# PEER stage of a diffusion layer on one core: three kinds of token tiles, one pass over v, gate rows on VectorE

## Chip, core and metric

The kernel runs on one core of one Trainium2 chip, in one launch. The metric is device microseconds of that core. All data are float32; large matrix products are done in three products of a high and a low part in fp32r. Matmuls run on TensorE, elementwise work on VectorE and ScalarE, row gathers are issued by GpSimd, all other transfers by SyncE's queue (SP).

## What is computed

The layer mixes tokens (neighbourhood attention beside a bidirectional recurrence) and then mixes channels in a PEER layer: each of 1024 tokens chooses, in each of 8 heads, 16 of 128 x 128 experts by product keys. An expert is a row of `u` and a row of `v`. Only this second part is changed.

```python
def peer(h, w_q, keys, u, v):
    q = (h @ w_q).reshape(B, S, PEER_HEADS, 2, PEER_HALF)
    s = jnp.einsum('bshpd,hpkd->bshpk', q, keys).astype(jnp.float32)
    top_s, top_i = lax.top_k(s, PEER_TOPK)
    cand_s = (top_s[..., 0, :, None] + top_s[..., 1, None, :]).reshape(B, S, PEER_HEADS, PEER_TOPK * PEER_TOPK)
    cand_i = (top_i[..., 0, :, None] * PEER_NKEYS + top_i[..., 1, None, :]).reshape(B, S, PEER_HEADS, PEER_TOPK * PEER_TOPK)
    best_s, pos = lax.top_k(cand_s, PEER_TOPK)
    expert = jnp.take_along_axis(cand_i, pos, axis=-1)
    gate = jax.nn.softmax(best_s, axis=-1).astype(h.dtype)
    def chunk(args):
        hc, ec, gc = args
        act = jax.nn.gelu(jnp.einsum('td,thkd->thk', hc, u[ec]))
        return jnp.einsum('thk,thkd->td', gc * act, v[ec])
```

## The kernel before

The 1024 tokens are 8 tiles of 128. Six tiles are **dense**: for them all 16384 experts are computed as matrix products, and the gates, zero for experts not chosen, pick the sum. Two tiles are **gathered**: each token's 128 chosen rows of u and of v are fetched one choice at a time (one indirect DMA on GpSimd brings one row of 1024 numbers to each of 128 tokens, 512 KB) and VectorE multiplies and sums them. `keep.y` holds the sum of a gathered tile.

Four stages run one behind the other, with all engines meeting between them: norms and attention, recurrence, merge with the routing projections (`project_and_route`, which leaves each tile's best scores and places in HBM), and then the two that matter here.

**Select** (`activate_and_select`) walks over 128 chunks of u, each the 128 experts that share a first index. For a chunk, SP loads u_raw (two buffers), ScalarE writes its high part u_hi, VectorE its low part u_lo (L1683), both in rings of three, and TensorE runs 48 matmuls of 384 tokens for the six dense tiles; ScalarE's gelu writes `a`, which goes to `act_scratch`. Beside that, by a schedule written out by hand (a lead of 12 chunks, six bodies of 18, a rest of 8), VectorE makes each tile's final choice in 8 parts (`Choice.part`), TensorE turns it, VectorE makes one-hot rows of it (`one2`, L1687, and `one1`, L1691, which carries the gate), and TensorE multiplies them in groups of four tokens into ps_g, the dense gates (L1895): 32 groups a tile, four in each of 8 chunks of a body. ScalarE copies them to `gm`, and SP stores them. VectorE also takes the rows of one gathered tile: 128 dot products with rows of u (L1806) and 128 additions of rows of v (L1810). Each frees one of four row buffers, for which GpSimd's next gather waits (L1620).

**Combine** (`combine`) walks over the 128 chunks of v twice, for three dense tiles each time, since 3 tiles x 2 halves are six of the eight PSUM banks. For a chunk, SP loads activations, gates and v_raw; VectorE multiplies gates by activations (L2035); ScalarE and VectorE make v_hi, v_lo (L2037), wa_hi and wa_lo (L2039); TensorE runs 18 matmuls of 512 columns into ps_y. Rings have four buffers: ScalarE's copy to v_hi waits until TensorE is done with the chunk four before. In pass 1 VectorE takes one u row of the second gathered tile per chunk (L2044), in pass 2 one v row (L2050); GpSimd fetches them (L1997). At the end of a pass the banks are copied out, turned and added to the residual (`finish`, L2063), 8 pieces a pass.

## Time and profile before

| what | us |
|---|---|
| median of three runs (3873.61 to 3875.75) | 3874.95 |
| span of the profiled execution | 3878.8 |
| select, first to last u matmul starts | 1524.0 to 2784.5 |
| combine, first to last v matmul starts | 2799.4 to 3868.4 |
| TensorE busy in the span | 3642.9 |
| VectorE busy | 2626.6 |
| GpSimd busy | 611.8 |

The profile is one execution; its span is 3.9 us above the median. Busy time counts overlapping instructions once, and consecutive instructions of one engine overlap a little: what one costs its engine is the distance to the start of the next. A matmul of 512 columns is listed with 0.39 us, though one begins every 0.23 us.

### The profile page before, as it was taken

How to read it: one execution, taken by the hardware profiler on the slowest of the kernel's cores; microseconds unless marked ns; L12 is line 12 of the kernel's file. 1: busy time of each engine (PE TensorE's matmuls, PEld its weight loads, DVE VectorE, ACT ScalarE, POOL GpSimd, SP SyncE). 2: the span in 40 equal slices, each digit the busy share in tenths (PEclk: the TensorE clock that was granted, in tenths of full speed). 3: DMA queues.
4: the chain of work that ended last, by engine and by line, in shares of the span. 5: the costliest groups of instructions: out<-in, count | busy, mean ns of one | idle time of the engine just before them, and what ended most of it. 6: DMA issues, size and time to landing. Idle time of an engine off the chain costs nothing. (4 is left out here: it accounts for less than half of the span.)

```text
span 3878.8 us, 57008 instructions
## 1 busy us (share of the span) xinstructions
PE 3642.9 (94%) x20360; PEld 3195.4 (82%) x20360; DVE 2626.6 (68%) x5328; ACT 1271.2 (33%) x1760; POOL 611.8 (16%) x516
## 2 busy tenths in 40 slices
PE   5899999799599896999999999999899999999999
PEld 2777777687487796999999999999878888878887
DVE  5134443488533786577878888888588888878887
ACT  3133343377311311222322232323233333333332
POOL 0000000000000000222232323132122222332221
PEclk8999999899799998999999999999999999999999
DMA  7311110111333112667777869595899999999997
GB/s 281 136 61 59 49 56 28 52 58 38 123 117 126 54 51 78 207 214 234 264 261 237 285 211 306 190 333 166 278 387 352 354 353 355 323 378 353 353 353 255
DMA packets 372666, 811.48 MB, mean 209 GB/s; under 512 B 30704, under 2 KB 207728, under 8 KB 369008
## 3 DMA queue, kind: packets, MB, share of 16 engines
q1 hardware_dynamic: 298736, 540.29, 39.8%
q0 software_dynamic: 73728, 268.47, 20.0%
q8 instruction: 130, 2.13, 0.2%
q14 instruction: 72, 0.59, 0.0%
HBM read 679.14 MB, written 129.50 MB: 208 GB/s over the span
## 5 line engine op out<-in xcount | busy, mean ns | idle before, releaser
L80 PE MATMUL s_ps_a<-back_dense_hi,s_u_hi 128*128 128x384 f32 x2048 | 703.2, 343 | 30.4 <-DVE s_u_lo L1683 30.4
L82 PE MATMUL s_ps_a<-back_dense_hi,s_u_lo 128*128 128x384 f32 x2048 | 686.2, 335 | 0.0
L81 PE MATMUL s_ps_a<-back_dense_lo,s_u_hi 128*128 128x384 f32 x2048 | 685.8, 335 | 0.0
L80 PE MATMUL c_ps_y<-c_v_hi,c_wa_hi 128*128 128x512 f32 x1536 | 601.1, 391 | 28.0 <-DVE c_wa_lo L2039 27.7
L81 PE MATMUL c_ps_y<-c_v_lo,c_wa_hi 128*128 128x512 f32 x1536 | 599.8, 391 | 0.0
L82 PE MATMUL c_ps_y<-c_v_hi,c_wa_lo 128*128 128x512 f32 x1536 | 599.6, 390 | 0.0
L2005 ACT ACTIVATE c_v_hi<-c_v_raw 128x1024 fp32r<-128x1024 f32 x256 | 271.5, 1060 | 633.3 <-PE c_ps_y L82 585.5
L1620 POOL DMA_INDIRECT s_row<-in_u_rows,back_expert x128 | 159.6, 1247 | 2004.2 <-DVE back_expert L1785 1582.7
L2037 DVE TENSOR_TENSOR c_v_lo<-c_v_raw,c_v_hi 128x1024 fp32r<-128x1024 f32 x256 | 313.4, 1224 | 181.8 <-ACT c_v_hi L2005 180.2
L80 PEld LDWEIGHTS s_ps_a<-back_dense_hi,s_u_hi 128*128 128x128 f32 x2048 | 386.1, 189 | 30.5 <-DVE s_u_lo L1683 30.5
L81 PEld LDWEIGHTS s_ps_a<-back_dense_lo,s_u_hi 128*128 128x128 f32 x2048 | 386.2, 189 | 0.0
L82 PEld LDWEIGHTS s_ps_a<-back_dense_hi,s_u_lo 128*128 128x128 f32 x2048 | 385.2, 188 | 0.0
L80 PEld LDWEIGHTS c_ps_y<-c_v_hi,c_wa_hi 128*128 128x128 f32 x1536 | 289.8, 189 | 89.8 <-DVE c_v_lo L2037 29.2
L82 PEld LDWEIGHTS c_ps_y<-c_v_hi,c_wa_lo 128*128 128x128 f32 x1536 | 289.7, 189 | 60.7
L81 PEld LDWEIGHTS c_ps_y<-c_v_lo,c_wa_hi 128*128 128x128 f32 x1536 | 289.9, 189 | 60.0
L1683 DVE TENSOR_TENSOR s_u_lo<-s_u_raw,s_u_hi 128x1024 fp32r<-128x1024 f32 x128 | 156.5, 1223 | 239.1 <-ACT s_u_hi L1639 223.4
L1643 ACT ACTIVATE s_a<-s_ps_a 128x768 f32<-128x768 f32 x128 | 103.9, 812 | 501.0 <-PE s_ps_a L82 487.8
L1657 ACT ACTIVATE s_gm<-s_ps_g 128x512 f32<-128x512 f32 x192 | 114.8, 598 | 399.0 <-PE s_ps_g L1895 399.0
L1620 POOL DMA_INDIRECT s_row<-in_v,back_expert x128 | 171.7, 1342 | 413.1 <-DVE back_y L1810 398.4
L1895 PE MATMUL s_ps_g<-s_one 128*128 128x128 f32 x1536 | 206.7, 277 | 6.7 <-DVE s_one L1691 6.7
L1691 DVE TENSOR_SCALAR s_one<-s_iota,s_sel_t 128x128 f32<-128x128 f32 x768 | 212.7, 349 | 0.0
L1895 PEld LDWEIGHTS s_ps_g<-s_one 128*128 128x128 f32 x1536 | 195.3, 191 | 20.6 <-DVE s_one L1691 20.4
(331 smaller groups left out, 6723.9 us busy)
## 6 DMA issues: line engine op xcount, KB each, us to landing
c_v_raw<-in_v SPq DMA_DIRECT2D x256, 512.0 KB
s_u_raw<-in_u SPq DMA_DIRECT2D x128, 512.0 KB
act_scratch<-s_a SPq DMA_DIRECT2D x128, 384.0 KB
gm_scratch<-s_gm SPq DMA_DIRECT2D x48, 1024.0 KB
c_a<-act_scratch SPq DMA_DIRECT2D x256, 192.0 KB
c_g<-gm_scratch SPq DMA_DIRECT2D x256, 192.0 KB
a_w<-in_w_ada SPq DMA_DIRECT2D x24, 1024.0 KB, 7.5
gate_scratch<-at_gate SPq DMA_DIRECT2D x32, 256.0 KB, 2.0
```

The lines of the kernel that those rows point to most:

```text
L80: nc.tensor.matmul(out, w_hi, x_hi, start=first, stop=False)
L81: nc.tensor.matmul(out, w_hi, x_lo, start=False, stop=False)
L82: return nc.tensor.matmul(out, w_lo, x_hi, start=False, stop=last)
L1620: gp.indirect_dma_start(out=row[:, n % R], out_offset=None, in_=io["u_rows"] if n < SEL else io["v_rows"], in_offset=bass.IndirectOffsetOn ...
L1643: nc.scalar.activation(a[:, s].rearrange("p (h t) -> p h t", h=2), ps_a[:, s, :, 0:W], ACT.Gelu_apprx_tanh).then_inc(act_done, 1)
L1657: nc.scalar.activation(gm[:, :, g * GT:(g + 1) * GT], ps_g[:, g % 2].rearrange("p (i t) -> p i t", t=GT), ACT.Copy).then_inc(g_copied, 1)
L1683: nc.vector.tensor_tensor(u_lo[:, n], u_raw[:, s], u_hi[:, n].bitcast(F32), ALU.subtract).then_inc(u_lo_done, 1)
L1691: last = nc.vector.tensor_scalar(one1[:, g % 2, i], iota[:], sel_t[:, 0, t:t + 1], sel_t[:, 2, t:t + 1], ALU.is_equal, ALU.mult)
L1895: last = nc.tensor.matmul(ps_g[:, g % 2].rearrange("p (n t) -> p n t", t=GT)[:, :, i], one2[:, g % 2, i], one1[:, g % 2, i], start=True, s ...
L2005: nc.scalar.activation(v_hi[:, s], v_raw[:, s], ACT.Copy).then_inc(v_hi_done, 1)
L2037: nc.vector.tensor_tensor(v_lo[:, s], v_raw[:, s], v_hi[:, s].bitcast(F32), ALU.subtract).then_inc(v_lo_done, 1)
```

## The change

The tiles are now of three kinds. Tiles 0 to 3 are dense in both stages (`BOTH = 4`). Tiles 4 and 5 are dense in select (their activations are among the 768 columns), but in combine their v rows are gathered: GpSimd looks up each chosen expert's activation with an indirect DMA of one 4-byte number a token from `act_scratch` (index `keep.place`), VectorE multiplies these by the gates (`weights`) and adds the rows (`unit`). Tiles 6 and 7 are gathered in both, and both of them now wholly in select: 2 x 128 dots, then 2 x 128 additions, by turns for the two tiles, with six row buffers.

Combine has one pass over v, with 4 tiles x 2 halves on all eight banks; v_hi, v_lo, wa_hi and wa_lo lie in the space of the dense tokens, which nobody needs any more. Gates are stored in blocks of 32 tokens and loaded for eight chunks at a time. All loops are written out. Select's work is placed by `selection_plan`, a table that gives each chunk its parts of choices, its gate groups and its number of rows. The end turns and finishes 16 pieces. `project_and_route` stores the choices tile by tile, in the order of `CHOICES`.

```diff
+BOTH = 4
+LOOKED = DENSE - BOTH
+TB = BOTH * P
+CHOICES = (6, 0, 7, 1, 2, 3, 4, 5)
...
-            for first, end, turn in ((DENSE, DENSE + 1, 0), (0, DENSE, 1), (DENSE + 1, TT, DENSE + 1)):
-                sp.dma_start(io["best_scr"][:, turn:turn + end - first], all_best[:, first:end]).then_inc(chosen_stored, 16)
...
+            for n, tile in enumerate(CHOICES):
+                sp.dma_start(io["best_scr"][:, n], all_best[:, tile]).then_inc(chosen_stored, 16)
...
+def selection_plan():
+    parts, turn, groups, rows = ([[] for _ in range(NK)] for _ in range(4))
+    begin = {0: (0, 2), 1: (4, 2), 2: (10, 1), 3: (20, 0.5), 4: (44, 0.5), 5: (72, 0.5), 6: (92, 0.5), 7: (108, 0.5)}
...
+    for g in range(BOTH * GROUPS):
+        groups[10 + g * 113 // (BOTH * GROUPS)].append(g)
+    units, taken = 2 * GATHERED * SEL, 0
+    span = [8.3 + 1.02 * len(groups[c]) for c in range(NK)]
+    other = [1.3 + 3.4 * len(parts[c]) + 2.15 * len(groups[c]) for c in range(NK)]
+    share = (sum(other) + 1.32 * units) / sum(span)
+    for c in range(NK):
+        fit = int((sum(span[:c + 1]) * share - sum(other[:c + 1])) / 1.32)
+        upto = units if c == NK - 1 else min(units, max(fit, taken)) if c >= 5 else 0
+        rows[c] = list(range(taken, upto))
+        taken = upto
+    return parts, turn, groups, rows, ends
...
+            for c in range(NK):
+                for d in turn[c - 1] if c >= 1 else ():
+                    turned_in(d)
+                for g in groups[c + 1] if c + 1 < NK else ():
+                    plain_rows(g)
+                first = len(rows[c]) // 2
+                for n in rows[c][:1]:
+                    unit(n)
+                if c + AHEAD < NK:
+                    low(c + AHEAD)
+                for n in rows[c][1:first]:
+                    unit(n)
+                for n, j in parts[c]:
+                    part(n, j)
+                for n in rows[c][max(first, 1):]:
+                    unit(n)
...
+            def look_up(b):
+                for n in range(b * BATCH, (b + 1) * BATCH):
+                    t, k = n % LOOKED, n // LOOKED
+                    gp.indirect_dma_start(out=looked[:, t, k:k + 1], out_offset=None, in_=table,
+                                          in_offset=bass.IndirectOffsetOnAxis(ap=keep.place[:, t, k:k + 1], axis=0)).then_inc(look_in[b % PHASES], 16)
...
+                    if n >= R:
+                        gp.wait_ge(used, n - R + 1)
...
+            look_up(0)
+            look_up(1)
+            for b in range(BATCHES):
+                fetch(b)
+                if b + 2 < BATCHES:
+                    look_up(b + 2)
...
+        units_upto = [0 if c < FIRST else UNITS * (c - FIRST + 1) // row_chunks for c in range(NK)]
...
+                nc.vector.tensor_tensor(spans, g[:, b % 2, :, i], spans, ALU.mult).then_inc(gated, 1)
+                dve.wait_ge(v_hi_done, c + 1)
                 nc.vector.tensor_tensor(v_lo[:, s], v_raw[:, s], v_hi[:, s].bitcast(F32), ALU.subtract).then_inc(v_lo_done, 1)
...
+                for n in here[:1]:
+                    unit(n)
+                dve.wait_ge(wa_hi_done, c + 1)
+                nc.vector.tensor_tensor(wa_lo[:, s], a[:, s], wa_hi[:, s].bitcast(F32), ALU.subtract).then_inc(wa_lo_done, 1)
+                for n in here[1:]:
+                    unit(n)
```

In combine `BATCH` is 16, `R` is 8, `FIRST` is 3, and `used` counts the rows that VectorE has added.

GpSimd's whole work in the two stages (s_ names a tile of select, c_ one of combine). Before:

```order
L1620 DMA s_row<-in_u_rows,back_expert 128x1024 x128
L1620 DMA s_row<-in_v,back_expert 128x1024 x128
L1512 UNCONDITIONAL_BRANCH
L1992 UNCONDITIONAL_BRANCH
L1997 DMA c_row<-in_u_rows,back_expert 128x1024 x128
L1997 DMA c_row<-in_v,back_expert 128x1024 x128
```

After, to the third batch of rows:

```order
L1634 DMA s_row<-in_u_rows,back_expert 128x1024 x256
L1634 DMA s_row<-in_v,back_expert 128x1024 x256
L1539 UNCONDITIONAL_BRANCH
L1958 UNCONDITIONAL_BRANCH
L1965 DMA c_looked<-act_scratch,back_place 128x1 x32
L1973 DMA c_row<-in_v,back_expert 128x1024 x16
L1965 DMA c_looked<-act_scratch,back_place 128x1 x16
L1973 DMA c_row<-in_v,back_expert 128x1024 x16
L1965 DMA c_looked<-act_scratch,back_place 128x1 x16
L1973 DMA c_row<-in_v,back_expert 128x1024 x16
```

256 gathers moved from combine to select, and combine got 256 look-ups between 256 row gathers, 32 of them ahead of the first row.

VectorE in combine, from one row to the next chunk's gate product, before (c_g is gates, c_v_lo and c_wa_lo the low parts):

```order
L2044 SCALAR_TENSOR_TENSOR c_row,c_dots<-c_row,c_tok 128x1024
L2035 TENSOR_TENSOR c_g<-c_g,c_a 128x384
L2036 REGISTER_ALU
L2037 TENSOR_TENSOR c_v_lo<-c_v_raw,c_v_hi 128x1024
L2039 TENSOR_TENSOR c_wa_lo<-c_g,c_wa_hi 128x384
```

and after, in chunks 3 and 4 (back_dense_lo and back_dense_hi now hold the low and high parts):

```order
L2031 TENSOR_TENSOR c_a<-c_g,c_a 128x512
L2033 TENSOR_TENSOR back_dense_lo<-c_v_raw,back_dense_hi 128x1024
L2002 TENSOR_TENSOR c_w<-c_looked,back_gate 128x2x8
L2014 SCALAR_TENSOR_TENSOR c_y<-c_row,c_w,c_y 128x1024
L2039 TENSOR_TENSOR back_dense_lo<-c_a,back_dense_hi 128x512
L2014 SCALAR_TENSOR_TENSOR c_y<-c_row,c_w,c_y 128x1024
L2031 TENSOR_TENSOR c_a<-c_g,c_a 128x512
```

A chunk carries two rows instead of one, and the first of them stands ahead of the low part that TensorE waits for.

VectorE in select, in a chunk with gate groups, before (s_one is one2 and one1):

```order
L1683 TENSOR_TENSOR s_u_lo<-s_u_raw,s_u_hi 128x1024
L1687 TENSOR_TENSOR s_one<-s_iota,s_sel_t 128x512
L1691 TENSOR_SCALAR s_one<-s_iota,s_sel_t 128x128 x4
L1804 ISA
L1806 ISA
L1806 SCALAR_TENSOR_TENSOR s_row,s_dots<-s_row,s_tok 128x1024
L1686 REGISTER_ALU
L1687 TENSOR_TENSOR s_one<-s_iota,s_sel_t 128x512
L1691 TENSOR_SCALAR s_one<-s_iota,s_sel_t 128x128 x4
```

and after, a chunk with one group and six rows:

```order
L1694 TENSOR_TENSOR s_one<-s_iota,s_sel_t 128x512
L1699 TENSOR_SCALAR s_one<-s_iota,s_sel_t 128x128 x4
L1803 SCALAR_TENSOR_TENSOR s_row,s_dots<-s_row,s_tok 128x1024
L1680 TENSOR_TENSOR s_u_lo<-s_u_raw,s_u_hi 128x1024
L1803 SCALAR_TENSOR_TENSOR s_row,s_dots<-s_row,s_tok 128x1024 x5
```

The groups, four in eight chunks of eighteen before, now stand one or two in every chunk from 10 to 122, made one chunk ahead of their matmuls.

## Rows read from the trace of the kernel before

**Rows 1.** The page's first line.
```profile
span 3878.8 us, 57008 instructions
```
**Rows 2.** Stages by tile: duration ns min/median/max, first and last start; who waited.
```profile
L80 PE MATMUL s_ps_a<-back_dense_hi,s_u_hi x2048: 334/334/689, 1524.0 to 2784.5; 128*128 128x384 f32 x187
...
L80 PE MATMUL c_ps_y<-c_v_hi,c_wa_hi x1536: 389/389/767, 2799.4 to 3867.9; 128*128 128x512 f32 x192
...
L82 PE MATMUL c_ps_y<-c_v_hi,c_wa_lo x1536: 387/389/628, 2800.4 to 3868.4; 128*128 128x512 f32 x192
...
  ACT c_v_hi L2005: 585.5, 228
```
**Rows 3.** Windows: length, busy us of PE, PEld, DVE, ACT, POOL; clock, DMA share, GB/s.
```profile
1524.00:2785.00 1261.00, 1254.26 (x7698) 1240.10 (x7698) 980.33 (x2137) 356.93 (x472) 331.36 (x256) 1.00 0.73 241
2800.00:2860.00 60.00, 53.79 (x219) 43.50 (x218) 46.52 (x73) 21.57 (x29) 14.24 (x15) 0.92 1.04 411
2820.00:2824.00 4.00, 0.07 (x1) 0.10 (x1) 1.91 (x3) 2.08 (x3) 0.00 (x0) 0.87 1.05 409
2824.00:2829.00 5.00, 5.00 (x12) 3.94 (x13) 5.00 (x9) 2.27 (x4) 1.59 (x2) 0.50 1.04 411
2900.00:3300.00 400.00, 400.00 (x1766) 331.24 (x1765) 324.28 (x491) 144.41 (x196) 99.23 (x98) 1.00 0.99 354
```
**Rows 4.** Timeline of VectorE in select: start us, us, what; idle before.
```profile
1545.19 1.23 DVE L1683 TENSOR_TENSOR s_u_lo<-s_u_raw,s_u_hi 128x1024 fp32r<-128x1024 f32 x1 [3.72 <-ACT s_u_hi L1639]
...
1553.51 1.22 DVE L1683 TENSOR_TENSOR s_u_lo<-s_u_raw,s_u_hi 128x1024 fp32r<-128x1024 f32 x1 [4.80 <-ACT s_u_hi L1639]
...
1716.04 1.23 DVE L1683 TENSOR_TENSOR s_u_lo<-s_u_raw,s_u_hi 128x1024 fp32r<-128x1024 f32 x1 [2.38 <-ACT s_u_hi L1639]
1717.18 0.68 DVE L1687 TENSOR_TENSOR s_one<-s_iota,s_sel_t 128x512 f32<-128x512 f32 x1
...
1718.81 1.22 DVE L1806 SCALAR_TENSOR_TENSOR s_row<-s_row,s_tok 128x1024 f32<-128x1024 f32 x1
...
1728.38 1.22 DVE L1683 TENSOR_TENSOR s_u_lo<-s_u_raw,s_u_hi 128x1024 fp32r<-128x1024 f32 x1 [2.31 <-ACT s_u_hi L1639]
```
**Rows 5.** Timeline of VectorE in combine, one chunk without waits.
```profile
2824.85 0.55 DVE L2035 TENSOR_TENSOR c_g<-c_g,c_a 128x384 f32<-128x384 f32 x1
2825.32 1.22 DVE L2037 TENSOR_TENSOR c_v_lo<-c_v_raw,c_v_hi 128x1024 fp32r<-128x1024 f32 x1
2826.45 0.55 DVE L2039 TENSOR_TENSOR c_wa_lo<-c_g,c_wa_hi 128x384 fp32r<-128x384 f32 x1
2826.92 1.22 DVE L2044 SCALAR_TENSOR_TENSOR c_row<-c_row,c_tok 128x1024 f32<-128x1024 f32 x1
...
2828.07 0.55 DVE L2035 TENSOR_TENSOR c_g<-c_g,c_a 128x384 f32<-128x384 f32 x1
```
**Rows 6.** Timeline of GpSimd (POOL) at the start of combine, and beside VectorE in select.
```profile
2790.91 0.94 POOL L1997 DMA_INDIRECT c_row<-in_u_rows,back_expert  x1 [0.30 <-issue]
...
1854.22 1.22 DVE L1806 SCALAR_TENSOR_TENSOR s_row<-s_row,s_tok 128x1024 f32<-128x1024 f32 x1
1854.57 1.68 POOL L1620 DMA_INDIRECT s_row<-in_u_rows,back_expert  x1 [4.43 <-DVE s_row L1806]
...
1855.36 2.28 DVE L1723 TENSOR_REDUCE s_sel<-s_work 128x128 f32<-128x2048 f32 x1
1856.55 0.94 POOL L1620 DMA_INDIRECT s_row<-in_u_rows,back_expert  x1 [0.30 <-issue]
```
**Rows 7.** Groups by line, GpSimd: busy us, mean ns, idle before and releasers.
```profile
L1620 POOL DMA_INDIRECT s_row<-in_v,back_expert x128 | 171.7, 1342 | 413.1 <-DVE back_y L1810 398.4 <-issue 12.5 <-DVE s_row L1806 2.1
L1620 POOL DMA_INDIRECT s_row<-in_u_rows,back_expert x128 | 159.6, 1247 | 2004.2 <-DVE back_expert L1785 1582.7 <-DVE s_row L1806 404.6 <-issue 17.0
```
**Rows 8.** Timeline of GpSimd in pass 2, one of a series of like rows.
```profile
3420.97 2.61 POOL L1997 DMA_INDIRECT c_row<-in_v,back_expert  x1 [0.66 <-DVE c_y L2050]
```
**Rows 9.** Timeline of the end: the eight finishes of VectorE.
```profile
3870.46 5.91 DVE L2063 SCALAR_TENSOR_TENSOR c_x<-c_ps_t,keep_mod,c_x 128x512 f32<-128x512 f32 x8 [0.95 <-PE c_ps_t L2127]
```
**Rows 10.** Timeline of SP's queue, one of six stores ending `project_and_route`.
```profile
1508.01 0.46 SPq L1300 DMA_DIRECT2D best_scratch<-p_x  x1
```

More of the change, by code:

```diff
@@ L1506, in activate_and_select @@
     W = TD // 2
-    LEAD_UNITS = 8
-    UNITS = [4 if j == PARTS or j >= HOT_END else 2 for j in range(BODY)]
-    PER_BODY = sum(UNITS)
-    HALF_BODIES = DENSE // 2
-    assert LEAD_UNITS + HALF_BODIES * PER_BODY == SEL and LEAD_UNITS == REST
+    UNITS = GATHERED * SEL
+    parts, turn, groups, rows, ends = selection_plan()
+    chunk_of = {g: c for c in range(NK) for g in groups[c]}
+    blocks = BOTH * P // SPAN
+    PER_BLOCK = SPAN // GT
     with ExitStack() as ctx:
@@ L1614, in _ @@
+            for b in range(2):
+                sp.wait_ge(a_stored[b], 16 * (NK // 2))
+                sp.wait_ge(g_stored[b], 16 * (blocks // 2))
         @block.gpsimd
         def _(gp):
-            gp.wait_ge(step, STEPS)
-            for n in range(2 * SEL):
+            for n in range(2 * UNITS):
+                if n < UNITS:
+                    g, k, table = n // SEL, n % SEL, io["u_rows"]
+                else:
+                    g, k, table = n % GATHERED, (n - UNITS) // GATHERED, io["v_rows"]
+                if n < UNITS and k == 0:
+                    gp.wait_ge(step, BEFORE[CHOICES.index(DENSE + g) + 1])
@@ L1842, in _ @@
-            for c in range(AHEAD):
-                lo(c, 0)
-            nc.vector.memset(keep.y[:], 0.0).then_inc(y_zero, 1)
-            dve.wait_ge(consts_in, 32)
-            choice = Choice(0, 0)
-            rows = Rows(0, 0, None)
-            for j in range(LEAD):
-                if j < PARTS:
-                    choice.part(j)
-                else:
-                    dve.wait_ge(tok_in, 16)
-                    rows.take(LEAD_UNITS // (LEAD - PARTS), True)
-                lo(j + AHEAD, 0)
@@ new lines, in selected @@
+            def selected(d):
+                pe.wait_ge(step, BEFORE[DENSE_CHOICES[d] + 1])
+                if d >= 1:
+                    pe.wait_ge(turned, d)
+                for r in range(3):
+                    last = nc.tensor.transpose(ps_t[:, r * P:(r + 1) * P], sel[:, r], ident[:])
+                last.then_inc(t_ready, 1)
+            pe.wait_ge(consts_in, 48)
+            for c in range(NK):
+                for q in range(4):
+                    quarter(c, q)
+                    if q == 1:
+                        for d in turn[c]:
+                            selected(d)
+                    if q in (1, 3):
+                        for g in groups[c][q // 2:q // 2 + 1]:
+                            gates(g)
@@ L1992, in _ @@
+            for k in range(KD):
+                for j in range(2):
+                    sp.wait_ge(out_done, 2 * k + j + 1)
+                    sp.dma_start(io["out"][:, k * T + j * HALF:k * T + (j + 1) * HALF], x1[j][:, k]).then_inc(stored, 16)
+            sp.wait_ge(stored, 16 * 2 * KD)
         @block.gpsimd
         def _(gp):
-            for n in range(2 * SEL):
-                if n >= RING:
-                    gp.wait_ge(used, n - RING + 1)
-                gp.indirect_dma_start(out=row[:, n % RING], out_offset=None, in_=io["u_rows"] if n < SEL else io["v_rows"],
-                                      in_offset=bass.IndirectOffsetOnAxis(ap=keep.expert[:, 1, n % SEL:n % SEL + 1], axis=0)).then_inc(row_in[n % RING], 16)
+            table = io["act_scr"].rearrange("c p (t o) -> (c p t) o", o=1)
@@ L2064, in finish @@
+            def finish(k, j):
+                n = 2 * k + j
+                dve.wait_ge(turned, n + 1)
+                nc.vector.scalar_tensor_tensor(out=x1[j][:, k], in0=ps_y[:, n % BANKS], scalar=keep.mod[:, 5 * KD + k:5 * KD + k + 1], in1=x1[j][:, k],
                                                op0=ALU.mult, op1=ALU.add).then_inc(out_done, 1)
             nc.vector.memset(y[:], 0.0).then_inc(y_zero, 1)
-            with dve.Fori(0, NK // RING) as i:
-                for s in range(RING):
-                    chunk(0, i, RING * i + s, s)
-                    dot(i, bass.ds(RING * i + s, 1), s)
```

843 lines of the change are left out of this document (357 added, 486 removed).

## The prediction

> **What bounds the kernel now.** I read the page's first lines, then where the two expert stages begin and end, then single stretches. The span is 3878.8 us [rows 1]. The select stage's matmuls run from 1524.0 to 2784.5, the combine stage's from 2799.4 to 3868.4, and in the latter ScalarE waits 585.5 us for TensorE to free a ring slot [rows 2]: data is there, TensorE is the bound. The windows agree: TensorE is busy for 400 of 400 us in the middle of combine, 1766 matmuls, 0.2265 us each; in select it is busy 1254 of 1261 us and VectorE 980 us [rows 3]. In select a chunk of u without gate matmuls takes 8.32 us (from one u_lo to the next), one with four gate groups 12.34 us, so a group of four gate matmuls costs TensorE 1.01 us [rows 4]. GpSimd only issues row gathers, one for each of 512 rows, and mostly waits for VectorE.
>
> **Part 1, combine on TensorE.** Before: two passes over v, 18 matmuls a chunk, 4608 in all. After: one pass, 4 tiles x 2 halves x 3 products = 24 a chunk, 3072. At 0.2265 us a chunk takes 5.44 us, the pass 696 us. If TensorE stayed the bound, this alone would take 1536 x 0.2265 = 348 us away.
>
> **Part 2, what must keep up in combine.** VectorE: starts of successive instructions give 0.47 us for 384 columns, 1.13 for 1024 and 1.15 for a row [rows 5]; 512 columns interpolate to 0.60. A chunk is gate product 0.60, v_lo 1.13, wa_lo 0.60 and 2.05 rows at 1.15, in sum 4.7 us, below 5.44. ScalarE's two copies a chunk are the same pieces of work, on an engine that waited before. Transfers: v 67.1 MB, activations 33.6, gates 33.6, 256 rows 134.2, x1 4.2, in sum 272.6 MB. Over 696 us that is 392 GB/s. The trace moves 411 GB/s over 60 us with the DMA share at 1.04, and 354 where it was only asked for that [rows 3]; at 411 the bytes take 663 us. 32768 look-ups of 4 bytes come on top. So DMA lies 0 to 5% below TensorE's pace, without air.
>
> The Trainium skill (DMA: Bandwidth & Descriptors, Specifications) gives some 358 GB/s as the limit of HBM for one core. By it the bytes would take 272.6 / 0.358 = 761 us, an estimate; this trace's 411 GB/s speak against it as a ceiling when one core runs.
>
> **Part 3, GpSimd in combine, where I choose.** It issued 256 gathers in 1079 us and now issues 512 (256 rows and 256 look-ups, one for each selected expert of tiles 4 and 5) in one queue, in batches of 16 and 16; I take a look-up to cost it what a row does, as both name 128 indices. Alone, a gather takes 0.94 us plus 0.30 us to the next, 1.24 [rows 6]. Beside VectorE it takes longer: one issued at 1854.57 into a row product that began at 1854.22 took 1.68 us, one issued beside a reduction with a single SBUF input 0.94 [rows 6]. The slow one ends 0.81 us after the end of that product, as if it had been let in only then; the product has two SBUF inputs. Over the 256 gathers of select the means are 1.247 and 1.342 us [rows 7], so 1.6 us from one to the next when nothing else holds it.
> All of VectorE's work in a combine chunk has two SBUF inputs, and it would be busy 4.7 of 5.44 us, about as much as in select. A pair of row and look-up then takes 3.2 us, while TensorE wants one in 5.44 / 2.05 = 2.65. So **GpSimd becomes the bound**. The ends: 2.48 us a pair if no gather waits, and 6.54 us if every one behaves like the stretch with 3.27 us each [rows 8]. I take 3.2, since select is the nearest stretch in VectorE's load; my own range for it is 2.9 to 3.6.
>
> The Trainium skill says the same in part (SBUF — State Buffer, Who interferes with whom): a VectorE instruction with two SBUF inputs contends with a GpSimd one that reads SBUF, and the later one blocks. It adds the inference that such instructions leave descriptor writing alone; by that a pair would stay near 2.5 us and TensorE would be the bound. The 1.68 us row speaks for a delay.
>
> The stage, from its first DMA issue (2789.2 before):
> - 32 look-ups ahead of the first row, 32 x 1.24 = 40 us. VectorE reaches a row in chunk 3 and TensorE stands there until about 46, but GpSimd is the one that counts.
> - 14 rounds of 16 rows and 16 look-ups, 448 x 1.6 = 717 us. VectorE needs 16 x 2.3 = 37 us of the 51 in a round. TensorE idles up to 9 us a round. Behind 4 us without matmuls (2820 to 2824) its granted clock was 0.50, that is 1.2 GHz, from 2824 to 2829 [rows 3]; a fall of 7 us a round costs 3 to 4 us, which still fits into 51.
> - the last 32 rows, no longer between look-ups, at VectorE's pace of 2.3 us: 74 us; about 4 us for a landing (an estimate, from 0 to 8) and 5.4 for TensorE's last chunk.
> Sum 40 + 717 + 74 + 9 = 840 us, where before it was 3868.6 - 2789.2 = 1079. **Combine: -239.**
>
> **Part 4, the end.** 16 banks instead of 8 are finished in a row behind the last matmul; 8 took 5.91 us [rows 9]. **+6.** The old finish in the middle of pass 2 is already in part 3's difference.
>
> **Part 5, select.** Only 4 tiles get gate rows: 128 groups for 192, so 64 x 1.01 = 65 us less on TensorE; 1261 becomes 1196. VectorE loses 64 x 1.63 = 104 us and gains 256 rows x 1.15 = 294 (tile 7's rows move here from combine): 980 + 190 = 1170 of 1196 us, 98%. Counting `selection_plan`'s table by these prices, no chunk leaves VectorE more than some 12 us behind, and u_lo is two chunks (17 us) ahead, so most of it is covered. What isn't: in chunks with two groups VectorE waits up to 5 us for TensorE's gates; 5.3 rows a chunk at 1.6 us ask 8.5 of GpSimd's 9.3 us; the last five chunks carry 31 rows, at 1.6 us 50 us where TensorE needs 42. Transfers are 419 MB, 351 GB/s. I give back 15 us. **Select: -50** (0 to -65).
>
> **Part 6, small ones.** 16 DMAs for 6 store the choices behind the last top-16, 0.46 us each [rows 10]: +4. The first gate load of combine is 2.1 MB; that is hidden behind the 32 look-ups, and would cost 3 us if they were not there. Start of select: +1.
>
> **Sum.** 3878.8 - 239 + 6 - 50 + 5 = 3601. The median of three runs, 3874.95, is 3.9 us below the profiled span; so 3597.
>
> **Rivals.**
> - *TensorE and DMA set combine, GpSimd hides.* For: GpSimd's 0.94; VectorE stands still when it lacks a row and then lets gathers pass. Against: the means of select. Stage: 46 us until chunk 3, then 125 x 5.44 = 680, and 0 to 35 us for DMA that runs at its limit: 726 to 761, against 1079 a gain of 318 to 353. Total 3483 to 3520. With 358 GB/s in place of 411 the stage is 761 + some 10 for the start, total 3530.
> - *Select loses its balance.* VectorE at 98% with waits on rows. Against: the two chunks of lead. If it runs 5% over its 1170 and combine is as forecast, total 3640; with GpSimd at 1.9 us a gather in combine as well (448 x 0.3 = 134) 3775.
> - *Slower than before: every gather waits behind a whole VectorE round.* Place: combine's row fetches. At 3.27 us each [rows 8], 512 take 1674 us, and the total is near 4500. It decides from (1079 + 39 - 123) / 448 = 2.2 us a gather on (the 39 us are what parts 4 to 6 save, 123 the parts of the stage not in the 448). For: a whole series of such gathers. Against: they stand only where VectorE had no gap at all; a starved VectorE has gaps.
> - *The change doesn't do what it says*: it is written out, nothing is left to a scheduler; below 1%.
>
> **Chances.** Forecast, 3530 to 3690: 0.54. TensorE or DMA bound, 3480 to 3530: 0.28. Select or GpSimd worse, 3690 to 3865: 0.14. Slower: 0.03. Within 0.2% (about what a measurement of this kernel can tell from no change): 0.01. So faster 0.96. The range 3475 to 3700 takes in the first two cases and a little of the third, about 0.83.
>
> **What would show it.** GpSimd busy over 75% in combine, its idle times "issue" and not VectorE's release; VectorE waiting for c_row; TensorE in combine busy about 83%, with the granted clock at half after gaps; last matmul some 840 us after the stage's first DMA. If instead ScalarE still waits for TensorE and gathers last 0.94 to 1.0 us, the rival has it. In select: matmuls over 1196 to 1215 us, few waits of TensorE for one-hot rows or u_lo. I am wrong above all if a look-up costs GpSimd or the DMA engines something else than a row.

## The result and the profile after

The changed kernel takes 3747.09 us (median of four runs, 3739.56 to 3749.73), the kernel before beside it 3875.35: a ratio of 0.9666, 95% interval 0.9652 to 0.9679, 128 us faster. The forecast was 3597, 278 us faster, with a range that ended at 3700. The direction was right, more than half of the gain did not come, and the time lies outside the range.

The profiled execution's span is 3737.8 us; the forecast in its terms was 3601, so 137 us are missing. (It is the fastest of the four: by the medians 150 are missing. What follows accounts for the 137.) The page's first line, then a row of the tile view of select (as in [rows 2]), then the windows of the two stages (as in [rows 3]):

```profile
span 3737.8 us, 47042 instructions
```

```profile
L84 PE MATMUL s_ps_a<-back_dense_hi,s_u_hi x2048: 333/334/689, 1521.3 to 2796.5; 128*128 128x384 f32 x187
```

```profile
1521.00:2797.00 1276.00, 1212.15 (x7180) 1203.93 (x7180) 1158.41 (x2193) 316.29 (x409) 719.78 (x505) 0.97 0.89 326
2900.00:3600.00 700.00, 568.17 (x2367) 463.92 (x2366) 473.10 (x509) 155.46 (x196) 572.90 (x411) 0.89 0.80 300
```

Select did not shrink: 1276 us, where [rows 2] give 1261. TensorE is busy for 1212 of it, VectorE for 1158 instead of 980. In combine TensorE is busy 568 of 700 us; GpSimd is busy 573, and with 0.30 us of issue before each of its 411 instructions (123 us) that fills the 700. The granted clock there is 0.89 for 1.00 before.

The end of select and the start of combine (timeline: VectorE's last row sums, ScalarE's last gelu, SP's first loads; the counterparts before were at 2785.27 and 2789.22):

```profile
2795.86 6.53 DVE L1814 SCALAR_TENSOR_TENSOR back_y<-s_row,s_w,back_y 128x1024 f32<-128x1024 f32 x5 [1.24 <-DMA s_row<-in_v,back_expert]
2797.26 0.81 ACT L1670 ACTIVATE s_a<-s_ps_a 128x768 f32<-128x768 f32 x1 [7.75 <-PE s_ps_a L86]
...
2804.55 6.42 DVE L1814 SCALAR_TENSOR_TENSOR back_y<-s_row,s_w,back_y 128x1024 f32<-128x1024 f32 x5 [0.56 <-DMA s_row<-in_v,back_expert]
2811.81 2.50 DVE L1814 SCALAR_TENSOR_TENSOR back_y<-s_row,s_w,back_y 128x1024 f32<-128x1024 f32 x2 [0.84 <-DMA s_row<-in_v,back_expert]
2816.56 0.37 SPq L1931 DMA_DIRECT2D c_g<-gm_scratch  x1
```

TensorE is through with u at 2796.9, VectorE still has some dozen rows to add, and combine's first load goes out 19.7 us after the last matmul instead of 4.3.

Groups by line (busy us, mean ns, idle before and its releasers): VectorE's rows in both stages, GpSimd's gathers (as in [rows 7]).

```profile
L1814 DVE SCALAR_TENSOR_TENSOR back_y<-s_row,s_w,back_y 128x1024 f32<-128x1024 f32 x256 | 319.2, 1281 | 49.3 <-DMA s_row<-in_v,back_expert 48.9
L1803 DVE SCALAR_TENSOR_TENSOR s_row<-s_row,s_tok 128x1024 f32<-128x1024 f32 x256 | 305.3, 1220 | 49.2 <-DMA s_row<-in_u_rows,back_expert 48.5
L2014 DVE SCALAR_TENSOR_TENSOR c_y<-c_row,c_w,c_y 128x1024 f32<-128x1024 f32 x256 | 326.7, 1278 | 262.9 <-DMA c_row<-in_v,back_expert 262.6
L1973 POOL DMA_INDIRECT c_row<-in_v,back_expert x256 | 389.0, 1520 | 80.1 <-issue 76.2 <-DVE c_y L2014 3.9
L1965 POOL DMA_INDIRECT c_looked<-act_scratch,back_place x256 | 332.7, 1300 | 87.0 <-issue 77.7 <-POOLq L1539 9.2
```

In combine GpSimd waits for VectorE 3.9 us in all, and VectorE waits 262.9 for rows: GpSimd's queue sets the stage, as forecast. In select VectorE waits 98.5 us for rows. That was not forecast. 1158, 98.5 and 16.5 for u_hi add up to 1273 of the stage's 1276.

The loss in select isn't spread out. From the first matmul of one chunk of u to that of the next, the 98 chunks with one gate group have a median of 9.23 us, those without a group 8.32 and those with two 10.04. The 127 such distances are 96 us longer than these prices add up to, and 94 of the 96 lie in 23 chunks. The longest, 21.0 us in the ninth chunk, is no wait for rows: TensorE stands there for the first tile's choice, which VectorE is still making (view of waits for TensorE in select: us in all, times, longest).

```profile
PE s_ps_t L1869 <- DVE s_sel L1787: 18.5, 4, 10.5
```

Where the 137 us lie: combine from its first load to its last matmul 906.0 for 840 (+66); select 1275.6 for 1211 (+65); the way from select's last matmul to combine's first load 19.7 for 4.3 (+15); the end 15.2 for 16.4 (-1); select's start 1521.3 for 1529 (-8).

### The profile page after: what moved, and what is told of

It reads as the page before. It is cut to its first block and busy times, and to the rows that moved or that the text cites. A ratio compares the mean times of both kernels' runs of the same rounds, so it can differ in the third digit from the quotient of the medians.

```text
span 3737.8 us, 47042 instructions
## 1 busy us (share of the span) xinstructions
PE 3276.6 (88%) x18306; PEld 2887.7 (77%) x18306; DVE 2580.4 (69%) x4897; ACT 1054.7 (28%) x1438; POOL 1450.4 (39%) x1028
## 5 line engine op out<-in xcount | busy, mean ns | idle before, releaser
L84 PE MATMUL c_ps_y<-back_dense_hi 128*128 128x512 f32 x1024 | 415.2, 406 | 190.7 <-DVE back_dense_lo L2039 190.7
L2014 DVE SCALAR_TENSOR_TENSOR c_y<-c_row,c_w,c_y 128x1024 f32<-128x1024 f32 x256 | 326.7, 1278 | 262.9 <-DMA c_row<-in_v,back_expert 262.6
L1634 POOL DMA_INDIRECT s_row<-in_v,back_expert x256 | 375.8, 1468 | 240.4 <-DVE back_y L1814 181.9
L1973 POOL DMA_INDIRECT c_row<-in_v,back_expert x256 | 389.0, 1520 | 80.1 <-issue 76.2
L85 PE MATMUL c_ps_y<-back_dense_lo,back_dense_hi 128*128 128x512 f32 x1024 | 411.6, 402 | 0.0
L86 PE MATMUL c_ps_y<-back_dense_hi,back_dense_lo 128*128 128x512 f32 x1024 | 410.7, 401 | 0.0
L1965 POOL DMA_INDIRECT c_looked<-act_scratch,back_place x256 | 332.7, 1300 | 87.0 <-issue 77.7
L1814 DVE SCALAR_TENSOR_TENSOR back_y<-s_row,s_w,back_y 128x1024 f32<-128x1024 f32 x256 | 319.2, 1281 | 49.3 <-DMA s_row<-in_v,back_expert 48.9
L1803 DVE SCALAR_TENSOR_TENSOR s_row<-s_row,s_tok 128x1024 f32<-128x1024 f32 x256 | 305.3, 1220 | 49.2 <-DMA s_row<-in_u_rows,back_expert 48.5
L85 PEld LDWEIGHTS c_ps_y<-back_dense_lo,back_dense_hi 128*128 128x128 f32 x1024 | 201.3, 197 | 42.2
```

The source lines that it names most:

```text
L84: nc.tensor.matmul(out, w_hi, x_hi, start=first, stop=False)
L85: nc.tensor.matmul(out, w_hi, x_lo, start=False, stop=False)
L86: return nc.tensor.matmul(out, w_lo, x_hi, start=False, stop=last)
L1634: gp.indirect_dma_start(out=row[:, n % R], out_offset=None, in_=table, in_offset=bass.IndirectOffsetOnAxis(ap=keep.expert[:, g, k:k + 1], ...
L1803: nc.vector.scalar_tensor_tensor(out=row[:, n % R], in0=row[:, n % R], scalar=1.0, in1=tok[:, g], op0=ALU.mult, op1=ALU.mult, accum_out=do ...
L1814: nc.vector.scalar_tensor_tensor(out=keep.y[:, g], in0=row[:, n % R], scalar=w[:, g, k:k + 1], in1=keep.y[:, g], op0=ALU.mult, op1=ALU.add ...
```

## Experiments

In all of them "stage" is combine from SP's first load to the last matmul, "step" the mean distance between the starts of the 33rd and the 481st gather, and "select" its first to its last matmul, all from the profiled execution. The changed kernel has 906, 1.72 and 1276 us. Runs that leave a stage as it is show how far these numbers move by themselves: combine 897 to 913 us with a step of 1.70 to 1.73 and 75 to 90 gathers of over 2 us, select 1269 to 1278.

**1. Combine without look-ups.**

```diff
-            look_up(0)
-            look_up(1)
...
-                if b + 2 < BATCHES:
-                    look_up(b + 2)
...
-                dve.wait_ge(look_in[b % PHASES], 16 * BATCH * (b // PHASES + 1))
-                nc.vector.tensor_tensor(w[:, :, cols], looked[:, :, cols], keep.gate[:, GATHERED:, cols], ALU.mult).then_inc(w_done, 1)
+                nc.vector.tensor_tensor(w[:, :, cols], keep.gate[:, GATHERED:, cols], keep.gate[:, GATHERED:, cols], ALU.mult).then_inc(w_done, 1)
```

> The 256 look-ups of activations in combine are left out (the weights of tiles 4 and 5 are then the gates squared, so their part of the sum is not the reference's). Measured in the changed kernel: the stage takes 906 us from its first SP issue to the last matmul, GpSimd starts one gather every 1.71 us and idles only by issue. Theory 1, GpSimd's queue sets the stage: 256 gathers at about 1.7 us are 435 us, far below TensorE's pace, so TensorE or the transfers bound the stage: 125 x 5.44 = 680 plus some 25 for the start and 5 for the end, 710 to 760 us, total 3750 - 170 = about 3580. Rival, TensorE and the 272 MB of transfers set it (the 4-byte look-ups carry no bytes): the stage stays above 870 us, total above 3710.

The stage takes 727 us, the total is 3568.7. Its window:

```profile
2900.00:3500.00 600.00, 600.00 (x2649) 496.82 (x2648) 540.33 (x578) 181.25 (x223) 341.76 (x229) 1.00 1.02 396
```

TensorE is busy for the whole 600 us at the full clock, as in [rows 3], and GpSimd now waits 300.8 us for VectorE to free a buffer. First to last matmul is 705 us, where the 128 chunks of 5.44 that the prediction's rival had for a bound are 696. So the look-ups, one number a token each, cost the changed kernel some 180 us. The run alone doesn't tell GpSimd's time from that of their 32768 descriptors; 396 GB/s with a DMA share of 1.02 in this run, against 300 and 0.80 in the changed kernel, show that the engines that move data were not the limit there, and experiment 2, with as many look-ups and a DMA share of 0.59 over the same 909 us, shows it from the other side. The 396 GB/s over 600 us also settle a point of the prediction: the Trainium skill's 358 GB/s for one core's HBM (DMA: Bandwidth & Descriptors, Specifications), which the page makes by halving a stack's rate between two cores, is no ceiling here, with one core running.

**2. Quarter rows: 128 KB a gather instead of 512, the same instructions.**

```diff
-                gp.indirect_dma_start(out=row[:, n % R], out_offset=None, in_=table,
+                gp.indirect_dma_start(out=row[:, n % R, 0:D // 4], out_offset=None, in_=table,
...
-                    gp.indirect_dma_start(out=row[:, n % R], out_offset=None, in_=io["v_rows"],
+                    gp.indirect_dma_start(out=row[:, n % R, 0:D // 4], out_offset=None, in_=io["v_rows"].rearrange("e (q d) -> (e q) d", q=4),
```

> In both stages every row gather brings 256 numbers a token in place of 1024 (128 KB for 512 KB; the rest of each row buffer is set to zero once, so the gathered sums are wrong); GpSimd issues the same instructions and VectorE works over the same 1024 columns. Select moves 218 MB for 419, combine 172 for 273. Select: theory 1, full DMA queues delay the loads of u (ScalarE waited 139.5 us for them, 3.4 before) and the rows: select falls from 1276 us to 1200 to 1220. Rival, VectorE's load and its fixed order make the waits: select stays at 1260 to 1276. Combine: theory 1, GpSimd's instruction count sets it: the stage stays at 906 us within 20. Rival, bytes set it: it falls below 840.

Combine: 909 us, of which GpSimd spent 9 waiting for the zeroes, with a step of 1.71. A hundred MB less change nothing. Select: 1203 us, inside the 1200 to 1220 of the first theory and 7 above what the prediction had before it gave 15 back. What became shorter is the landing (DMA issues of select, last number the median us from issue to landing; first the changed kernel, then this one), and with it VectorE's waits (groups of this one):

```profile
s_row<-in_u_rows,back_expert POOLq DMA_INDIRECT x256, 8.0
```

```profile
s_row<-in_u_rows,back_expert POOLq DMA_INDIRECT x256, 4.0
```

```profile
L1817 DVE SCALAR_TENSOR_TENSOR back_y<-s_row,s_w,back_y 128x1024 f32<-128x1024 f32 x256 | 317.6, 1284 | 4.2 <-DMA s_row<-in_v,back_expert 4.1
L1806 DVE SCALAR_TENSOR_TENSOR s_row<-s_row,s_tok 128x1024 f32<-128x1024 f32 x256 | 302.6, 1217 | 12.7 <-DMA s_row<-in_u_rows,back_expert 12.4 <-DVE s_digit L1768 0.2
```

**3. Quarter vector: row products and sums over 256 columns, whole transfers.**

```diff
-                nc.vector.scalar_tensor_tensor(out=y[:, t], in0=row[:, n % R], scalar=w[:, t, k:k + 1], in1=y[:, t],
+                nc.vector.scalar_tensor_tensor(out=y[:, t, 0:D // 4], in0=row[:, n % R, 0:D // 4], scalar=w[:, t, k:k + 1], in1=y[:, t, 0:D // 4],
```

and the same in select's two forms.

> In both stages VectorE's row products and row sums work over 256 columns instead of 1024 (about 0.35 us for 1.15; the gathered sums are wrong), and every transfer is whole. With quarter rows and whole VectorE work select took 1203 us. Theory 1, transfers set what was lost in select: it stays at 1250 to 1276 us although VectorE loses 512 x 0.8 = 410 of its 1158 us. Rival, VectorE's load and order are needed for it as well: select falls to 1200 to 1220 here too. Combine: VectorE's busy time falls by 205 us, so that fewer gathers come up in a two-input instruction: the step falls from 1.72 to 1.4 to 1.6 us and the stage to 780 to 850; if GpSimd doesn't depend on VectorE it stays at 906.

Select falls to 1193 us, so the rival of this text was right: late rows without VectorE's load (1193 us) cost select next to nothing, and neither does the load without late rows (1203 us in experiment 2). VectorE waits even longer for rows here (232 us), but has the time. The loss needs both, an engine without slack and rows that come late to it. Combine falls to 762 us with a step of 1.41: GpSimd's pace hangs on what VectorE does.

**4. Three buffers for u_raw.**

```diff
-        u_raw = m.sb("u_raw", [P, 2, KD, P])
+        u_raw = m.sb("u_raw", [P, 3, KD, P])
...
-                if c + 4 < NK:
-                    u_load(c + 4)
+                if c + 5 < NK:
+                    u_load(c + 5)
```

> Select gets three buffers for u_raw instead of two, and SP asks for a chunk five ahead instead of four; nothing else changes. Theory 1, what costs select its 65 us is the late landing of single loads of u (ScalarE waited for them 139.5 us, up to 5.9 at a time, with the next load asked for only when VectorE had finished with the buffer two before): a third buffer takes most of these waits, select falls from 1276 us to 1215 to 1240, total 3690 to 3715. Rival 1, the queues simply lack throughput in the stretches with six rows a chunk: the loads wait as long as before, select stays within 10 us. Rival 2, it is the rows, not u, on which VectorE falls behind: within 10 us too, but with ScalarE's wait for u gone and VectorE's wait for rows (48.5 and 47.2 us) grown.

3732.66 us, ratio 0.9634 (0.9611 to 0.9656). Select takes 1262 us, 13 less and 7 below the shortest of the runs that leave it alone; ScalarE's waits for u fall from 139.5 us to 35.1, VectorE's for rows from 97 to 84. The late loads of u, the most visible wait in select's view of waits, were a sign of the same slow landings and not the cause. Rival 2 is nearest, though the rows' waits did not grow.

**5. and 6. Four and eight row buffers in select.**

```diff
-    R = 6
+    R = 4
```

> Select's ring of row buffers has 4 in place of 6; nothing else changes. Measured with 6: VectorE is busy 1158 us of select's 1276 and waits 98 us for rows; a row lands 8.0 to 8.4 us after its gather is issued (4.0 to 4.3 with quarter rows, where the waits for rows were 17 us and select 1203). Theory 1, VectorE is the bound of select and loses what it waits for rows, and that wait comes from landing time over the number of buffers: a buffer's turn is about 1.5 (issue) + 8.2 (landing) + 1.2 (VectorE) = 10.9 us, so 6 give a row every 1.8 us at best, 4 one in 2.7; 512 rows then take 1390 us at least where 1276 - 65 us are there for them: select 1400 to 1460 us, total 3870 to 3930. Rival, the lack is in the engines that move the bytes: fewer rows in flight land earlier, and select stays within 30 us of 1276.

```diff
-    R = 6
+    R = 8
```

> Select's ring of row buffers has 8 in place of 6; nothing else changes. Theory 1 (VectorE bounds select, and waits for rows because of landing time over buffers): with 8 a row can come every 1.4 us, VectorE's waits for rows fall from 98 us to 30 to 50, and select from 1276 us to 1215 to 1240; the additions behind the last matmul of u keep their number, so the gap of 19.7 us shrinks by 2 to 5; total 3695 to 3720. Rival, the transfers as a whole are the limit (the queues are busy 0.86 to 0.97 there): two more rows in flight only land later, 9 us and more, u comes later as well, and select stays within 15 us of 1276.

With 4 the total is 3988.7, slower than before the change, and select takes 1506 us. With 8 it is 3675.37 us, ratio 0.9479 (0.9465 to 0.9494), 72 us below the changed kernel, and select takes 1213, two us from the forecast. VectorE's two groups of rows with 4 buffers, then with 8:

```profile
L1814 DVE SCALAR_TENSOR_TENSOR back_y<-s_row,s_w,back_y 128x1024 f32<-128x1024 f32 x256 | 322.2, 1279 | 177.0 <-DMA s_row<-in_v,back_expert 176.4
L1803 DVE SCALAR_TENSOR_TENSOR s_row<-s_row,s_tok 128x1024 f32<-128x1024 f32 x256 | 307.7, 1220 | 157.1 <-DMA s_row<-in_u_rows,back_expert 155.8 <-issue 0.8
```

```profile
L1814 DVE SCALAR_TENSOR_TENSOR back_y<-s_row,s_w,back_y 128x1024 f32<-128x1024 f32 x256 | 318.0, 1280 | 12.2 <-DMA s_row<-in_v,back_expert 9.6 <-issue 1.4 <-DVE back_y L1814 1.1
L1803 DVE SCALAR_TENSOR_TENSOR s_row<-s_row,s_tok 128x1024 f32<-128x1024 f32 x256 | 303.4, 1217 | 22.1 <-DMA s_row<-in_u_rows,back_expert 17.8 <-issue 4.1
```

The waits go 334, 98.5, 34 us with 4, 6 and 8 buffers and select goes with them: 230 us more for 236 more of waiting, 62 less for 64 less. The chunks that take over 1 us more than their price are 64, 23 and 6. The engines that move the bytes had room for it: select's window with 8 reads 343 GB/s at a share of 0.92, where it was 326 at 0.89. The first theory stands, with its numbers off: I had expected select at 1400 to 1460 for 4 buffers and at 1215 to 1240 for 8, with a total of 3695 to 3720 and 2 to 5 us off the gap in front of combine, which lost 1. The gap in front of combine is still 18.6 us; VectorE has 13 sums left behind the last matmul of u, nearly without a wait among them. That part is the place of the rows in `selection_plan`, not their landing.

**7. Combine's v_lo by another instruction.**

```diff
-                nc.vector.tensor_tensor(v_lo[:, s], v_raw[:, s], v_hi[:, s].bitcast(F32), ALU.subtract).then_inc(v_lo_done, 1)
+                nc.vector.scalar_tensor_tensor(out=v_lo[:, s], in0=v_raw[:, s], scalar=1.0, in1=v_hi[:, s].bitcast(F32),
+                                               op0=ALU.mult, op1=ALU.subtract).then_inc(v_lo_done, 1)
```

> In combine VectorE makes v_lo by SCALAR_TENSOR_TENSOR (1.0 times v_raw, minus v_hi) in place of TENSOR_TENSOR: same numbers, same length. In the changed kernel a gather beside no VectorE instruction takes 0.94 us, one that comes up in the row product or in wa_lo 1.4 to 1.5 (it ends 0.81 us after the end of that instruction), and one that comes up in the gate product, with v_lo right behind it, 2.63: it is held through both. There are about 100 of these. Theory 1, only two TENSOR_TENSOR in a row hold a gather through both: the 2.63 turns to 1.5, GpSimd saves 100 x 1.15 = 115 us, less what VectorE's starving takes back; stage 906 to 800 to 840, total 3640 to 3680. Rival, any two instructions with two SBUF inputs back to back can hold it: no change within 10 us.

Ratio 0.964 (0.9622 to 0.9658), stage 888 us, step 1.68. Gathers of over 2 us are 72 instead of 88, and those that meet gate product and v_lo still last 2.63 (median of 84 of them). So the theory falls: with a SCALAR_TENSOR_TENSOR as the second instruction a gather is still held through two. The 18 us, more than the rival's 10, go with a smaller count of the same; of them only 9 lie outside what combine does by itself.

**8. A row between gate product and v_lo.**

```diff
-                dve.wait_ge(v_hi_done, c + 1)
-                nc.vector.tensor_tensor(v_lo[:, s], v_raw[:, s], v_hi[:, s].bitcast(F32), ALU.subtract).then_inc(v_lo_done, 1)
                 here = range(taken, units_upto[c])
                 taken = units_upto[c]
                 for n in here[:1]:
                     unit(n)
+                dve.wait_ge(v_hi_done, c + 1)
+                nc.vector.tensor_tensor(v_lo[:, s], v_raw[:, s], v_hi[:, s].bitcast(F32), ALU.subtract).then_inc(v_lo_done, 1)
```

> In combine VectorE's first row of a chunk stands between the gate product and v_lo in place of behind v_lo; nothing else changes. Theory 1, as for the kernel with v_lo by SCALAR_TENSOR_TENSOR: the gate product is followed by a SCALAR_TENSOR_TENSOR, the gathers of 2.63 us go down to 1.5, and the stage falls from 906 us by up to 115, total 3640 to 3690. Rival 1, the hold isn't of this kind: no change within 10 us. Rival 2, v_lo now stands behind a wait for a row, so that TensorE, which waits for v_lo, stops more often: the stage grows.

Ratio 0.9671 (0.9653 to 0.9688), stage 912 us, 90 gathers of over 2 us. The long ones only moved: they now stand over v_lo and wa_lo, which had come together (1.2 and 0.6 us, 2.63 to the end of the gather as before). No gain.

**9. One SBUF input for gate product, v_lo and wa_lo.**

```diff
-                nc.vector.tensor_tensor(spans, g[:, b % 2, :, i], spans, ALU.mult).then_inc(gated, 1)
+                nc.vector.tensor_copy(spans, g[:, b % 2, :, i]).then_inc(gated, 1)
...
-                nc.vector.tensor_tensor(v_lo[:, s], v_raw[:, s], v_hi[:, s].bitcast(F32), ALU.subtract).then_inc(v_lo_done, 1)
+                nc.vector.tensor_copy(v_lo[:, s], v_raw[:, s]).then_inc(v_lo_done, 1)
```

and wa_lo likewise.

> In combine VectorE's gate product, v_lo and wa_lo become plain copies of one SBUF input (g, v_raw and a), so the numbers are not the reference's; the row sums still have two inputs. Theory 1, an instruction of VectorE with two SBUF inputs holds a gather that comes up in it until its end: the gathers of over 2 us (88 of 512) vanish and only those that meet a row sum last 1.4 to 1.5; the mean falls from 1.41 us to 1.05 to 1.2, the step between gathers from 1.72 to 1.35 to 1.5, and the stage from 906 us to 740 to 800. Rival, what holds a gather is something else that was only beside these instructions (the queue's own room, or transfers): the mean stays at 1.35 or more and the stage above 880. If the copies are much shorter than the operations they replace, part of a gain is their shorter time; the durations by what runs beside a gather tell.

The stage falls to 856 us and the step to 1.61, gathers of over 2 us to 33: 50 us less, where 106 to 166 were expected, and between the two theories' ranges. The timeline says why (VectorE and GpSimd, beside two look-ups):

```profile
2830.14 0.69 DVE L2033 CAST back_dense_lo<-c_v_raw 128x1024 fp32r<-128x1024 f32 x1 [0.24 <-ACT back_dense_hi L1990]
2830.37 1.28 POOL L1965 DMA_INDIRECT c_looked<-act_scratch,back_place  x1 [0.30 <-issue]
...
2831.95 0.95 POOL L1965 DMA_INDIRECT c_looked<-act_scratch,back_place  x1 [0.30 <-issue]
```

The look-up that comes up in the copy, which has one input, ends 0.82 us behind the copy's end, as one behind a product does. The copies also run at nearly double pace (0.69 for 1.22 us). So one input is no protection; these copies only hold a gather more briefly. The Trainium skill (SBUF — State Buffer, Who interferes with whom) says that of copies and casts between places in SBUF in their fast modes, and this run agrees. The same section takes it that a `tensor_tensor` leaves descriptor writing alone; the rows below show a delay, and the measurement decides.

**10. Batches of four in combine; 11. the same and eight row buffers; 12. batches of two and eight row buffers.**

```diff
-    BATCH = 16
+    BATCH = 4
```

> In combine look-ups and rows go in batches of 4 in place of 16: 8 look-ups stand ahead of the first row instead of 32, and 8 rows behind the last look-up instead of 32. Measured before this: 42.8 us for the first 32 gathers, 1.72 us for each of 448, 92.9 us for the last 32 rows and the end (2.9 a row). Theory 1, GpSimd's queue sets the stage by a fixed step: 8 x 1.3 + 496 x 1.72 + 8 x 2.9 = 887 us for 906, total about 3730; less if rows that come evenly let VectorE and TensorE run evenly. Rival, in long batches VectorE stands still during the look-ups and lets them pass at 1.24 us, and with short ones every gather meets a working VectorE: the step grows to 1.85 or more, the stage to 940 or more, total 3780.

3707.31 us, ratio 0.9561 (0.9545 to 0.9577), stage 870 us, step 1.67; the 36 us are about twice what a fixed step gave (19). Gathers of over 2 us are 40 instead of 88.

> Eight row buffers in select, and batches of 4 look-ups and rows in combine: both edits together. They lie in different stages with a meeting of all engines between, so both theories expect their gains to add: combine as with batches of 4 alone, 870 us for 906, and select as with eight buffers alone. With select at 1215 to 1240: total 3650 to 3680; by the rival for select 3700 to 3710.

3646.61 us, ratio 0.9395 (0.9381 to 0.9409): select 1211, stage 876. The gains add, to 100 us where the two alone give 112.

```diff
-    R = 6
+    R = 8
...
-    BATCH = 16
+    BATCH = 2
...
-    PHASES = 4
+    PHASES = 8
```

> Eight row buffers in select, and batches of 2 look-ups and 2 rows in combine, with eight semaphores for the look-ups in place of four. Theory 1: what batches of 4 won (step 1.72 to 1.67, the last 32 gathers and the end 92.9 to 66 us) goes a little further, since 4 rows stand behind the last look-up for 8: combine 860 to 870 us, total 5 to 10 us below the version with batches of 4. Rival: the weights, now 128 small instructions of VectorE in place of 64, each behind a landing, make up for it or more: 0 to 15 us above.

3614.86 us, ratio 0.9322 (0.9307 to 0.9336), the fastest version here and 132 us below the changed kernel. The stage takes 838.5 us with a step of 1.60, and no gather at all lasts over 2 us. GpSimd's two groups in this version (tile view: min/median/max in ns):

```profile
L1973 POOL DMA_INDIRECT c_row<-in_v,back_expert x256: 940/1146/1893, 2762.2 to 3584.8; - x128
...
L1965 POOL DMA_INDIRECT c_looked<-act_scratch,back_place x256: 943/1433/1970, 2757.2 to 3577.9; - x128
```

I had put 10 us on going from 4 to 2; it brought 32. What the batches change is less the pauses at both ends than the way in which gathers and VectorE's chunk meet. It is a trade, though: of the 512 gathers 150 take 0.93 to 0.97 us in this version, where the changed kernel has 247.

**What a gather meets.** Laying the changed kernel's two timelines over each other from 2830 to 3700 us: 194 gathers with nothing of VectorE in their first 0.94 us take 0.94 to 0.96. A hundred that meet the gate product and v_lo behind it have a median of 2.63. Those that meet a row sum with wa_lo have 1.49, those with v_lo and a row sum 1.43. The rows of three of these kinds (VectorE, then GpSimd):

```profile
3204.23 1.27 DVE L2014 SCALAR_TENSOR_TENSOR c_y<-c_row,c_w,c_y 128x1024 f32<-128x1024 f32 x1
...
3210.16 0.68 DVE L2031 TENSOR_TENSOR c_a<-c_g,c_a 128x512 f32<-128x512 f32 x1
3210.76 1.21 DVE L2033 TENSOR_TENSOR back_dense_lo<-c_v_raw,back_dense_hi 128x1024 fp32r<-128x1024 f32 x1
3211.89 1.27 DVE L2014 SCALAR_TENSOR_TENSOR c_y<-c_row,c_w,c_y 128x1024 f32<-128x1024 f32 x1
...
3214.89 0.68 DVE L2031 TENSOR_TENSOR c_a<-c_g,c_a 128x512 f32<-128x512 f32 x1
3215.49 1.21 DVE L2033 TENSOR_TENSOR back_dense_lo<-c_v_raw,back_dense_hi 128x1024 fp32r<-128x1024 f32 x1
```

```profile
3204.83 1.48 POOL L1973 DMA_INDIRECT c_row<-in_v,back_expert  x1 [0.30 <-issue]
...
3210.50 2.28 POOL L1973 DMA_INDIRECT c_row<-in_v,back_expert  x1 [0.66 <-DVE c_y L2014]
...
3214.90 2.63 POOL L1965 DMA_INDIRECT c_looked<-act_scratch,back_place  x1 [0.30 <-issue]
3179.34 0.95 POOL L1965 DMA_INDIRECT c_looked<-act_scratch,back_place  x1 [0.30 <-issue]
```

The first came up in the row sum that ended at 3205.50 and ended 0.81 us later; the second came up in the gate product and ended 0.81 us after v_lo, at 3212.78. The third, of 2.63 us, began with the gate product and ended 0.83 us after v_lo.

That it is not just any work of VectorE shows in select of the same trace: 44 gathers that came up in one of the TENSOR_SCALARs that make one-hot rows (one SBUF input, 128 columns) took 0.94 us, while 76 that came up in u_lo (two inputs, 1024 columns) had a median of 1.68.

Why v_lo keeps out a gather that waited through the gate product, while a row sum behind wa_lo lets it in, stays open: in experiments 7 and 8 the long holds ended where a row sum began, whatever stood before it. Nor does the pair as such decide. In experiment 3, whose row sums are short, v_lo stands as close behind the gate product, and there 49 gathers that came up in the gate product were let in between the two, against 6 that were held to the end of v_lo. One of the 49:

```profile
3103.77 0.68 DVE L2031 TENSOR_TENSOR c_a<-c_g,c_a 128x512 f32<-128x512 f32 x1
3104.37 1.22 DVE L2033 TENSOR_TENSOR back_dense_lo<-c_v_raw,back_dense_hi 128x1024 fp32r<-128x1024 f32 x1
```

```profile
3104.19 1.07 POOL L1973 DMA_INDIRECT c_row<-in_v,back_expert  x1 [0.30 <-DVE c_y L2014]
```

It ended at 3105.26, 0.81 us after the gate product, with v_lo already under way.

## Why the prediction failed, by its steps

- **Part 1 and 2, TensorE, VectorE, transfers in combine**: right. 5.44 us a chunk is what experiment 1 shows as soon as nothing else holds, at 396 GB/s where 392 were asked for. The rival "TensorE and DMA set combine" describes that run (stage 726 to 761; measured 727), not the changed kernel.
- **Part 3, GpSimd becomes the bound**: right, and named by its sign beforehand (idle times "issue"; VectorE waiting for c_row; TensorE busy about 83%, measured 81 to 83). The size was 66 us off. The first 32 look-ups took 42.8 us for 40. The 448 gathers took 770 for 717, since the step was 1.72 and not 1.60: this is the term that failed. I had carried over the means of select, 1.25 to 1.34, though the rows of 2.61 us [rows 8] showed what back-to-back chunk work does, and in combine gate product and v_lo stand together in every chunk. The 88 gathers of over 2 us go with the difference: with batches of two they are gone and the step is 1.60. VectorE's busy share was the wrong guide: it is 0.68 in combine, below the 0.78 of the select from which the price came, and the gathers still took longer. The last rows and the end took 92.9 us for 83.
- **Part 4, the end**: +6 forecast, +4.8 measured.
- **Part 5, select**: failed, -50 forecast, +15 measured. Its terms for the engines held: a chunk with one group takes 9.23 us for 9.33, and VectorE is busy 1158 for 1170. With eight buffers select takes 1213 for 1211, but that near a hit is luck in part: the chunks at their own prices add up to 1180, not 1196, and 13 to 15 us go to the one wait for the first tile's choice, which the prediction didn't have. The step that failed is "no chunk leaves VectorE more than some 12 us behind, and u_lo is two chunks (17 us) ahead, so most of it is covered". It set VectorE's work against TensorE's and GpSimd's, but not the ring: six buffers, each in turn for issue, landing and product, some 11 us, give a row every 1.8 us at best; the chunks without parts of choices carry 5.3 rows in 9.2 us on average, one every 1.7, and a chunk with six rows wants them in 7. VectorE at 98% had little to make up for such waits with: they come to 98.5 us, and select is 80 us (the 15 given back and the 65 missing) above 1196. With eight buffers 34 us of waits go with 17 above it.
- **The gap**: the prediction had 8 us for the last five chunks' rows, inside the 15. The stage ends when VectorE does, 19.7 us behind TensorE, +15; experiment 6 leaves 18.6 of it with the sums coming nearly without a wait, which points to the plan; no run moved the rows to show it.
- **Part 6, the start**: +5 forecast, -3 measured; in the twelve kernels of the experiments select began at 1523.9 to 1528.5 with the same instructions ahead of it, so a few us there are no finding.
- **Rivals and range**: "select loses its balance" was the right place, and "waits on rows" stood in it, but its time came from VectorE running 5% over its 1170 us, which it did not (1158), and its 3640 doesn't come out of its own numbers: 5% over 1170 is 1229, 18 above the 1211, total 3615; the case "select or GpSimd worse", 3690 to 3865, had 0.14 and holds the result. The range left it out: it allowed 15 us for a plan with 2% of slack, in which nothing could go better than planned.

## What to carry over

An engine planned at 96 to 98% needs its inputs early, not on average: divide what a turn of a buffer costs (here 11 us, 8 of it landing under load) by the number of buffers, and compare the time per row that this gives with the densest stretch of the plan, not with its mean. One more buffer pair was worth 72 us here, more than any reordering. And where GpSimd's instructions are the bound, count how long each is held by what the other engine runs at that place, and try short batches of them: going from 16 to 4 brought 40 us here, and from 4 to 2 (with eight row buffers in select) 32.
